# The pooling branch of a hybrid mixer computed inside the delta rule instead of in a stage of its own

## The reference, cut to what matters

```python
def pool_mixer(p, pool_w, pool_scale):           # p: (1, 1024, 256), 4 groups of 64 channels
    pg = p.reshape(B, S, POOL_GROUPS, POOL_GROUP_DIM).astype(F32)
    ...
    for gi, win in enumerate(POOL_WINDOWS):      # windows 2, 4, 8, 16: trailing mean
        start = jnp.maximum(t + 1 - win, 0)
        cnt = (t + 1 - start).astype(F32)
        cs_g = cs[:, :, gi, :]
        means.append((cs_g[:, 1:] - cs_g[:, start]) / cnt[None, :, None])
    delta = (jnp.stack(means, axis=2) - pg).astype(p.dtype)
    mixed = jnp.einsum('bsgc,gcd->bsgd', delta, pool_w)
    return mixed.reshape(B, S, POOL_WIDTH) * pool_scale

def hybrid_mixer(...):
    proj = h @ w_in
    c_q, c_kv, k_rope, gq, gk, gv, gz, ga, gb, p = split_sizes(proj, IN_SIZES)
    y_mla = mla_attention(...)                   # 512 wide
    y_gdn = gdn_mixer(...)                       # gated delta rule in chunks of 64 tokens, 256 wide
    y_pool = pool_mixer(p, pool_w, pool_scale)   # 256 wide
    return jnp.concatenate([y_mla, y_gdn, y_pool], axis=-1) @ w_out
```

## Time and profile before

| what | value |
|---|---|
| time, median of 3 runs | 3734.45 us (3728.82 to 3736.33) |
| profiled execution | 3733.14 us |
| its span, first to last instruction | 3731.3 us |
| mean granted TensorE clock | 0.964 of full |
| PE busy | 3429.4 us (92% of the span) |
| DVE busy | 1622.8 us (43%) |
| ACT busy | 816.1 us (22%) |
| moved by DMA | 818.40 MB, mean 219 GB/s |

### The profile page before, as it was taken

The page is one execution under the profiler, slowest core; times in us unless marked ns, Lnnn a source line. Parts: engine busy times, 40 slices in busy tenths (PEclk is TensorE's granted clock), DMA queues, the critical chain, the costliest instruction groups (busy, mean ns, idle before and its releaser), DMA issues. The chain is left out here.

```text
span 3731.3 us, 51620 instructions
## 1 busy us (share of the span) xinstructions
PE 3429.4 (92%) x20918; PEld 1748.6 (47%) x20918; DVE 1622.8 (43%) x2561; ACT 816.1 (22%) x1811; POOL 364.8 (10%) x355
## 2 busy tenths in 40 slices
PE   7999999899999799999997999997999968897996
PEld 3444565433333344777654333333555658553332
DVE  3760886511111575777755011113333874463114
ACT  0000660100000123555501000001333542111112
POOL 1000300210000000000001100000000900003110
PEclk9999999899999999999998999998999979999998
DMA  9980211599999622000024999997213200419996
GB/s 383 359 313 1 92 69 68 223 411 427 425 423 423 234 80 77 5 1 1 1 102 194 396 426 425 427 421 287 98 70 113 102 1 4 169 71 351 419 419 265
DMA packets 146709, 818.40 MB, mean 219 GB/s; under 512 B 29891, under 2 KB 35651, under 8 KB 100390
## 3 DMA queue, kind: packets, MB, share of 16 engines
q1 hardware_dynamic: 117494, 737.20, 49.6%
q0 software_dynamic: 25808, 68.88, 4.8%
q10 hardware_dynamic: 3168, 8.96, 0.6%
HBM read 752.52 MB, written 82.55 MB: 224 GB/s over the span
## 5 line engine op out<-in xcount | busy, mean ns | idle before, releaser
L2289 PE MATMUL m_yp<-m_w,m_hidT 128*32 128x512 f32 (+2 forms) x2248 | 379.2, 596 | 11.9 <-issue 6.0
L2266 PE MATMUL m_up<-m_w,m_xT 128*32 128x512 f32 (+2 forms) x1792 | 303.9, 604 | 20.8 <-DMA m_w<-in_moe_w_up 20.8
L2266 PE MATMUL m_gp<-m_w,m_xT 128*32 128x512 f32 (+2 forms) x1792 | 300.7, 598 | 9.1 <-DMA m_w<-in_moe_w_gate 4.9
L2047 DVE TENSOR_TENSOR m_hid<-m_sg,m_up 128x512 f32<-128x512 f32 x42 | 28.9, 688 | 572.5 <-PE m_up L2266 572.5
L2042 DVE TENSOR_TENSOR m_yt<-m_yp,keep_flat 128x512 f32<-128x512 f32 x128 | 82.4, 686 | 400.5 <-PE m_yp L2289 394.1
L419 PE MATMUL front_acc<-front_hT,front_wt 128*128 128x512 f32 x512 | 224.0, 598 | 7.2 <-DMA front_wt<-in_na_w_qkv 7.2
L2289 PEld LDWEIGHTS m_yp<-m_w,m_hidT 128*32 128x32 f32 (+2 forms) x2248 | 122.0, 124 | 221.2 <-issue 216.0
L2266 PEld LDWEIGHTS m_up<-m_w,m_xT 128*32 128x32 f32 (+2 forms) x1792 | 104.3, 126 | 214.8 <-issue 214.8
L2347 ACT ACTIVATE m_sg<-m_gp 128x512 f32<-128x512 f32 (+1 forms) x64 | 33.5, 524 | 776.8 <-PE m_gp L2266 540.4
L2266 PEld LDWEIGHTS m_gp<-m_w,m_xT 128*32 128x32 f32 (+2 forms) x1792 | 97.6, 124 | 206.0 <-issue 202.8
L1202 PE MATMUL n_acc<-n_wt,n_hT 128*128 128x512 f32 (+2 forms) x512 | 191.1, 529 | 1.8 <-DMA n_wt<-in_w_in 1.1
(11 more groups left out here) (503 smaller groups left out, 5020.7 us busy)
## 6 DMA issues: line engine op xcount, KB each, us to landing
m_w<-in_moe_w_gate SPq DMA_DIRECT2D x64, 2048.0 KB
m_w<-in_moe_w_up SPq DMA_DIRECT2D x64, 2048.0 KB
m_w<-in_moe_w_down SPq DMA_DIRECT2D x64, 2048.0 KB
v<-in_ada_w SPq DMA_DIRECT2D x40, 1024.0 KB, 12.4
m_w<-in_moe_w_gate SPq DMA_DIRECT2D x32, 1024.0 KB
m_w<-in_moe_w_up SPq DMA_DIRECT2D x32, 1024.0 KB
m_w<-in_moe_w_down SPq DMA_DIRECT2D x32, 1024.0 KB, 31.7
v<-in_w_mod SPq DMA_DIRECT2D x24, 1024.0 KB, 11.1
```

What stands on the lines that cost most here:

```text
L2266: last = pe.matmul(acc[part, 0:F], xT[:, j, k, part], w[:, place_of[m_, r][0], k * F:(k + 1) * F], start=k == 0, stop=k == KC - 1)
L2289: last = pe.matmul(yp[e][part, :], hidT[:, k, part], w[:, place_of["d", r][0], k * D + e * 512:k * D + (e + 1) * 512], start=k == 0, stop= ...
```

## The change

pool_mix is gone as a stage; what it computed is done inside gdn. The diff, cut to its core:

```diff
-def pool_mix(nc, name, proj, first, a, w, scale, mixT, ahead):
...
-def gdn(nc, name, padded, first, a, mixT, room, flat_room, held, past_keys):
+def gdn(nc, name, padded, first, a, mixT, room, flat_room, held, past_keys, keys, dec, pooled, w_pool, ahead):
...
+        past = past_keys[:, :, :].rearrange("p h s -> p (h s)")
+        pp = past[:, 2048:4096].rearrange("p (t n) -> p t n", t=TILES)
+        band = past[:, 4096:5632].rearrange("p (d g s) -> p d g s", d=3, g=G)
...
+        turned_bank = lambda f, g: 4 + g + 2 * f
...
+            @block.sync
+            def _(sp):
+                after_uw, after_mt, after_mq = ahead
+                sp.wait_ge(uw_done[1], 1)
+                loads = [(pp, rows(pooled)), (band, a["pool_band"]), (psc, a["pool_scale_cols"])]
+                loads += [(pw[half(b)], w_pool[b::2].rearrange("a c d -> c a d")) for b in range(2)]
+                for dst, src in loads:
+                    sp.dma_start(dst, src).then_inc(pool_in, 16)
+                for dst, src in after_uw:
+                    sp.dma_start(dst, src).then_inc(ahead_in, 16)
+                for f in range(2):
+                    sp.wait_ge(mt_ready[f], 2)
+                for dst, src in after_mt:
+                    sp.dma_start(dst, src).then_inc(ahead_in, 16)
+                sp.wait_ge(mq_done[1], 1)
+                sp.wait_ge(z_ready, 2)
+                for dst, src in after_mq:
+                    sp.dma_start(dst, src).then_inc(ahead_in, 16)
+                sp.wait_ge(ahead_in, 16 * (len(after_uw) + len(after_mt) + len(after_mq)))
...
+                def copy_means(u):
+                    act.wait_ge(pd_done, u + 1)
+                    if u >= 2:
+                        act.wait_ge(pm_done, u - 1)
+                    act.activation(pdT[:, u % 2], ps[:, u % 2], ACT.Copy).then_inc(pd_cp, 1)
+
+                def scale_pooled(u):
+                    act.wait_ge(pm_done, u + 1)
+                    for j in range(G // 2):
+                        last = act.activation(mixT[:, 5 + 2 * j, 2 * u * P:(2 * u + 2) * P], ps[:, 2 + u % 2, 2 * P * j:2 * P * (j + 1)],
+                                              ACT.Copy, scale=psc[:, j:j + 1])
+                    last.then_inc(pm_scaled, 1)
+
+                act.wait_ge(pool_in, 16 * 5)
+                copy_means(0)
+                out_squares(0)
+                copy_means(1)
+                out_roots(0)
+                scale_pooled(0)
+                copy_means(2)
+                scale_pooled(1)
+                out_squares(1)
+                copy_means(3)
+                out_roots(1)
+                scale_pooled(2)
+                scale_pooled(3)
...
+                def means(u):
+                    if u >= 2:
+                        pe.wait_ge(pd_cp, u - 1)
+                    for t in (2 * u, 2 * u + 1):
+                        for j in range(G // 2):
+                            at_ = (t % 2 * 2 + j) * P
+                            for back in range(2 if t else 1):
+                                for g in (2 * j, 2 * j + 1):
+                                    last = pe.matmul(ps[half(g % 2), u % 2, at_:at_ + P], pp[:, t - back, g * C:(g + 1) * C],
+                                                     band[:, back if t else 2, g], start=back == 0, stop=back == 1 or t == 0)
+                    last.then_inc(pd_done, 1)
+
+                def pool_groups(u):
+                    pe.wait_ge(pd_cp, u + 1)
+                    if u >= 2:
+                        pe.wait_ge(pm_scaled, u - 1)
+                    for g in range(G):
+                        side = half(g % 2)
+                        o = ps[side, 2 + u % 2, g // 2 * 2 * P:(g // 2 + 1) * 2 * P].rearrange("p (t s) -> p t s", s=P)
+                        means_of = pdT[side, u % 2].rearrange("p (t a s) -> p t a s", t=2, s=P)[:, :, g // 2]
+                        last = pe.matmul(o, pw[side, g // 2], means_of, start=True, stop=True)
+                    last.then_inc(pm_done, 1)
...
+                pe.wait_ge(pool_in, 16 * 5)
+                means(0)
+                means(1)
+                pool_groups(0)
+                means(2)
+                pool_groups(1)
+                means(3)
+                turn_out(0)
+                pool_groups(2)
+                pool_groups(3)
+                turn_out(1)
...
+                homes = [keys[:, n * D:(n + 1) * D] for n in range(6)] + [dec[:, n * D:(n + 1) * D] for n in range(2)]
+                w_loads = list(zip(homes, a["w_out_2"][0].rearrange("(c p) n -> c p n", p=P)))
+                gdn(nc, "gdn", padded, AT_GDN, a, mixT, keep["raw"], keep["flat"], held, k2, keys, dec, proj[:, AT_POOL:AT_POOL + 256], a["pool_w_2"][0],
+                    (w_loads[0:4] + w_loads[6:] + loads[0:4], w_loads[4:6], loads[4:]))
+                out_norm(nc, "n4", lambda k: homes[k], wr, given, x4, alpha_2, x5, h5, keep, mixT, place=lambda k: 2 * k if k < 4 else 2 * k - 7,
+                         room=k2, x_room=held["early"][:, 0:TILES * D])
```

More of the change, by code:

```diff
@@ L1608, in norm_loads, with out_norm @@
     return list(zip(given, sources)) + [(wr, w_router.rearrange("(c p) n -> p c n", p=P))]
-def out_norm(nc, name, wt, wr, given, x, alpha, x_out, h_out, keep, srcT, place=lambda k: k, room=None):
+def out_norm(nc, name, weight_of, wr, given, x, alpha, x_out, h_out, keep, srcT, place=lambda k: k, room=None, x_room=None):
     KC, HALF, TURN = D // P, D // 2, 3
@@ L2397 @@
 GDN_HELD = {"early": [11776], "z": [TILES, GDN_W], "square": [6, P], "small": [8, 64], "ab": [TILES, 2 * GDN_H], "al": [GDN_H], "dtb": [GDN_H], "og": [64]}
-def pool_mix(nc, name, proj, first, a, w, scale, mixT, ahead):
[L2403 to L2445, removed]
-            @block.scalar
-            def _(act):
-                for t in range(TILES):
-                    act.wait_ge(d_done, t + 1)
-                    if t >= 2:
-                        act.wait_ge(m_done, t - 1)
-                    act.activation(dT[:, t % 2], dps[t % 2][0:C, 0:G * P].rearrange("c (g s) -> c g s", g=G), ACT.Copy).then_inc(cp, 1)
-            @block.vector
-            def _(dve):
-                dve.wait_ge(l_in, 64)
-                for t in range(TILES):
-                    dve.wait_ge(m_done, t + 1)
-                    dve.tensor_tensor(mixT[:, 5:8:2, t * P:(t + 1) * P], mps[t % 2][:, 0:W].rearrange("p (j s) -> p j s", j=2),
-                                      sc[:, :].unsqueeze(2).to_broadcast([P, 2, P]), ALU.mult).then_inc(scaled, 1)
@@ L2552, in gdn @@
         res_turned = [st.sem(f"res_turned{f}") for f in range(2)]
+        pool_in, ahead_in, pd_done, pd_cp, pm_done, pm_scaled = (
+            st.sem(n) for n in ("pool_in", "ahead_in", "pd_done", "pd_cp", "pm_done", "pm_scaled"))
         o_done, o_sq, o_sum, o_inv, o_rn, o_scaled, out_ready = (
@@ L2806, in _, with out_squares @@
                         act.activation(res[:, 2 * b:2 * b + 2].rearrange("p t n -> p (t n)"), ps[:, 4 + b], ACT.Copy).then_inc(inner_ready, 1)
-                for g in range(2):
+                def out_squares(g):
                     act.wait_ge(o_ready, 3 + 2 * g)
@@ L2999, in _, with turn_out @@
                         pe.sem_inc(o_done, 1)
-                for g in range(2):
+                def means(u):
[19 more added lines that the diff above has]
+                    last.then_inc(pm_done, 1)
+                def turn_out(g):
                     pe.wait_ge(out_ready, g + 1)
@@ L3039, in pool_bands @@
     s, t = np.arange(P)[:, None], np.arange(P)[None, :]
-    for g, win in enumerate((2, 4, 8, 16)):
+    for g, win in enumerate(POOL_WINDOWS):
         inside = (s <= t) & (s > t - win)
```

33 lines of the change are left out of this document (17 added, 16 removed).

## The result

The changed kernel takes 3711.93 us (median of 4 runs, 3710.28 to 3715.46), the kernel before 3735.39 in the same session (4 runs, 3728.82 to 3736.33): ratio 0.9943, 95% interval 0.9930 to 0.9955. That is 23.5 us less, where 26.4 were forecast. The profiled execution took 3712.36 us.

What follows compares the result with a forecast made beforehand. Stages follow behind barriers, so time removed between two comes off the end; the delta rule's end is a DVE chain. Sum: -29.3 + 1.7 - 0.9 + 2.1 = -26.4 us against 3734.45, giving 3708 us, range 3701 to 3716.

Steps and rivals of the forecast that it cites:

- The stage's removal: Pool stage between delta rule and output stage: the whole stage goes, -29.3 us.
- The products, packed: Moved means products in the delta rule's tail: alternating array halves, 0.055 us a record, 10.4 us of PE in all.
- The tail: DVE's chain at the delta rule's end: copies of means on ACT delay square by 1.4, root by 1.7 us.
- The second turn: Second output turn on PE: full clock instead of half, 1.09 us for 1.97, -0.9 us; other bound 0.
- The output stage's cold clock: Opening of the output stage without clock-keeping products: part of it at half clock, +2.1 us.
- The loads: Pool stage's 8.9 MB, issued once the uw products end: price zero, hidden by the chain of states, then DVE's tail.
- the loads slow the chain of states: Rival: PE's instruction fetches come late beside the 8.9 MB, five by 1.6 us each, 8 us, 3716; chance 0.09.

Runs made afterwards that it cites:

- e3: Changed kernel with ACT's order turned: out_squares(0) ahead of copy_means(0), out_roots(0) ahead of copy_means(1); 3707.59 us, ratio 0.9935.
- e0: The changed kernel itself, unaltered, run again on another set's chip for comparison; 3712.91 us, ratio 0.9946.
- e5: Changed kernel with three clock-keeping products ahead of the second output turn and one behind it; 3708.38 us, ratio 0.9937.
- e9: e8 with the 6.9 MB of loads for the next stage let go three states sooner; 3708.15 us, ratio 0.9926.
- e10: e5 with four transposes behind the second turn in place of the clock-keeping product; 3712.46 us, ratio 0.9939.
- e11: e7 with one clock-keeping product behind the second turn; 3710.33 us, ratio 0.9932.
- e2: Kernel before, with only the changed kernel's 8.9 MB of loads added in its delta rule, all loaded again later; 3739.08 us, ratio 1.0021.
- e7: e6 with pooled columns loaded at the delta rule's start and the band once its memory is free; 3705.04 us, ratio 0.9927.
- e1: Changed kernel with the 6.9 MB of next-stage loads waiting for the last state, pooled loads still early; 3714.64 us, ratio 0.9949.
- e4: Changed kernel with three clock-keeping products ahead of the second output turn; 3710.92 us, ratio 0.9943.
- e6: Changed kernel with the edits of e1 and e3 together; 3708.28 us, ratio 0.9937.
- e8: e7 with the second square right behind copy_means(1) and one clock-keeping product behind the second turn; 3710.53 us, ratio 0.9931.

## Why the prediction was right, and where it was off

**Forecast 3708 (3701 to 3716), measured 3711.9**, and faster, as said. By its steps:

- *The stage's removal* was right: PE has no wait for pool_in in the profile, and the 29.3 us are gone in full.
- *The products, packed*: right. 32 records in 1.97 us, 0.055 each; a pool_groups 1.08 where 0.9 was worked out, beside DVE's work and without effect.
- *The tail*: right in mechanism and size. Square 1.5 us later (1.4 forecast), root 1.76 (1.7), the table load just ahead of it. e3 shows the cause: with the order changed and all else kept, the root is back to within 0.1 us of where it was, and the second group to within 0.4.
- *The second turn*: mechanism right, size off: -0.3 of the -0.9. The turn took 1.63 us in the first profile, 1.09 in that of e0, whose opening then pays more (13.37 us for its first 24 records): the clock falls during this turn or just behind it, and what the turn gains the opening loses.
- *The output stage's cold clock*: +2.0 for +2.1, but the same opening cost 2.9 in e0, so that the size agrees is in part luck. Short stretches (columns of the earlier trace rows) show half clock from the second turn on; it ends at 3190.3, after 6.8 us, of which 3.8 lie in the output stage:

```profile
3183.00:3184.00 1.00, 0.97 (x6) 0.97 (x7) 0.73 (x2) 0.00 (x0) 0.00 (x0) 0.71 0.00 0
3184.00:3187.00 3.00, 1.19 (x5) 0.76 (x4) 1.06 (x2) 0.60 (x1) 0.00 (x0) 0.50 0.00 0
3187.00:3188.00 1.00, 1.00 (x2) 0.34 (x1) 0.77 (x2) 0.00 (x0) 0.00 (x0) 0.50 0.78 66
3188.00:3190.00 2.00, 2.00 (x3) 0.68 (x2) 0.00 (x0) 0.00 (x0) 0.00 (x0) 0.50 0.88 354
```

  e5, e9, e10 and e11 keep full clock through the opening.
- *The loads*: this step failed. "Price zero; what hides it is the chain of states" looked only for who waits for the data, and the chain of states was called a cover while it was the path itself. It cost 4.9 us. The rival "the loads slow the chain of states" had the mechanism, with a chance of 0.09 and 8 us for five blocks 1.6 us late each; in fact two blocks of the five came late enough to stop PE, by 2.9 and 2.1 us. Its point against, that the pool stage's fetches under full load did no harm, rested on one block: of the two in the earlier trace rows, one came at 3182 to 3183, at 88 GB/s and beside clock-keeping products, and only the other, 22 us later, under full load. That stage used few instructions, 184 matmuls in 20 us where the chain has 752 in 25, so a block could come late there and stop nothing.

The Trainium skill ("Runtime: NRT & Kernel Launch", Instruction fetch mechanics) has the fetch of a 16 KiB block mostly hidden. The traces agree where the DMA engines are idle: the chain of the kernel before has one spell by issue, 0.45 us. Under some 400 GB/s they don't: spells of 1.4 to 2.9 us in the chains.

Why was the time near the forecast all the same? With +4.9 and the other small differences the sum is -21.0, 3713.4 against the 3734.45 of before; the measured median lies 1.5 under that, within the spread of the runs. The miss of one term is a fifth of the gain and was inside the range, whose upper end came from that very rival.

What is shown and what is argued: that traffic in the chain makes the spells is shown (e2, and e7 without it). That they are late instruction blocks is argued, from where the packets of that queue lie, in all kernels as in the one above. In e7, 3161.4 to 3161.6, with PE going on at 3163.75, and in e9, 3164.6 to 3164.8, with PE going on at 3166.88:

```profile
q8 instruction: 1, 0.02, 30.0%
```

```profile
q8 instruction: 1, 0.02, 30.1%
```

No run made blocks smaller or gave them a queue with right of way, so how far ahead PE asks, and where in the DMA engines the request waits, stay open.

## What to carry to other kernels

A transfer that nobody waits for is not free when the engine on the path issues many small instructions: look at how often its instruction queue has a packet, and price the late blocks before you call a busy stretch of PE a cover. Big loads did no harm beside few, long instructions (the pool stage of before); where there is no such stretch, as here, expect the stall to follow them.

When work is put on an in-order engine (ACT here), put it behind the square, the table load or whatever the chain needs next: the same copies cost 1.8 us at the tail's end when ahead of it, and 0.4 behind it (0.1 at the root).

Split a busy stretch's time into idle spells and clock before you compare two profiles of it: here the same chain lay between 22.7 and 31.6 us by these two together.

## What the hardware showed unexpectedly

- Under the loads at about 400 GB/s, PE stood still for 1.4 to 3.7 us at a time, waiting for nothing that the profile shows (2.92 and 2.13 in the changed kernel, 2.65 and 2.13 in e2, 2.36 in e7, 3.67 in e9). In each of the 22 spells PE went on 2.2 to 2.7 us after one instruction block of 0.02 MB had gone over its queue.
- Half clock can follow such a spell: the 29 records behind the one of e7 took 3.18 us, those behind e1's 1.80. Half clock also comes without one: the chain of the kernel before is at half clock from 3148.4 to 3151.8.
- The clock at the opening of the output stage. With nothing between the second turn and a pause of 1.81 us it fell in all seven profiles: ahead of the opening in the changed kernel, e0 and e1, and 0.1 to 0.5 us behind it in e3, e4, e6 and e7 (12.23 us for 24 records in these four). With one product or four transposes behind the turn and a pause of 1.18 or 1.37 us it held in all four (10.54, in e5, e9, e10 and e11). In e8 the product stood there too, but the pause was 3.74 us, and the clock fell 1.3 us behind the opening.
